# Two reorderings in the recurrence of the odd layer: one on TensorE's queue, one on ScalarE's

## The reference, cut to what matters

```
def _odd_mixer(h_ctx, h_lat, w_in, lower_bounds, layer, out_norm, ctx_out):
    fq, f_fwd, f_bwd, fi, fog = _split(h @ w_in, ODD_SIZES)
    q = _heads(jax.nn.silu(fq), HGRN_HEADS)
    ...
    for d, f in enumerate((f_fwd, f_bwd)):
        log_f = jnp.logaddexp(jnp.log(lb[d]), jnp.log1p(-lb[d]) + jax.nn.log_sigmoid(...f...))
        k = -jnp.expm1(log_f)
        dirs.append(_directional_scan(q, k, i, log_f, n_ctx, reverse=(d == 1)))
    o_lat = _gated_readout(dirs[0][1] + dirs[1][1], og[:, :, n_ctx:], out_norm)
```

## Time and profile before

| | |
|---|---|
| median of three runs | 3188.07 us |
| the profiled execution | 3188.07 us |
| its span, first to last instruction | 3186.1 us |
| TensorE busy | 3034.2 us, 95% of the span |
| VectorE busy | 731.6 us, 23% |
| ScalarE busy | 414.7 us, 13% |
| GpSimd busy | 245.7 us, 8% |
| granted TensorE clock, mean | 0.978 of 2.4 GHz |

### The profile page before, as it was taken

The page is one execution under the profiler, slowest core; times in us unless marked ns, Lnnn a source line. Parts: engine busy times, 40 slices in busy tenths (PEclk is TensorE's granted clock), DMA queues, the critical chain, the costliest instruction groups (busy, mean ns, idle before and its releaser), DMA issues.

```text
span 3186.1 us, 41136 instructions
## 1 busy us (share of the span) xinstructions
PE 3034.2 (95%) x17920; PEld 1710.6 (54%) x17920; DVE 731.6 (23%) x1717; ACT 414.7 (13%) x1014; POOL 245.7 (8%) x322
## 2 busy tenths in 40 slices
PE   6988889999989999899988999989999999999998
PEld 2455644444448888577656777454444444444434
DVE  1037822000035666400032000243000000000002
ACT  1015220000022222200031000131000000000001
POOL 1022300000011122100000000000000000000030
PEclk9999989999999999999999999999999999999999
DMA  8670012122122222243343333326999999999993
GB/s 348 256 279 24 1 66 80 40 99 79 40 62 67 53 63 65 85 168 115 143 172 119 139 139 154 115 85 255 365 399 378 385 400 380 381 403 381 381 404 134
DMA packets 211812, 613.32 MB, mean 192 GB/s; under 512 B 6252, under 2 KB 53580, under 8 KB 205104
## 3 DMA queue, kind: packets, MB, share of 16 engines
q1 hardware_dynamic: 204912, 592.20, 49.0%
q0 software_dynamic: 6256, 17.87, 1.7%
q10 hardware_dynamic: 464, 0.60, 0.1%
HBM read 603.43 MB, written 7.21 MB: 192 GB/s over the span
## 4 chain that ended last, share of the span: by engine, by line
PE 91%; DVE 4%; DMA 2%; issue 1%; ACT 1%; POOLq 0%; POOL 0%; ACTq 0%; DVEq 0%
PE ps_ffn_gate L618 10%; PE ps_ffn_up L618 10%; PE ps_ffn_down L654 10%; PE ps_odd L1921 7%; PE ps_moe_down L3097 6%; PE ps_moe_up L3047 6%; PE ps_moe_gate L3047 6%; PE ps_lin L1408 4%; PE ps_moe_down L3104 3%; PE ps_project L536 3%; PE ps_moe_gate L3052 3%; PE ps_moe_up L3052 3%; PE ps_lin L300 3%; PE ps_odd L1944 2%; PE ps_mod L1331 1%
## 5 line engine op out<-in xcount | busy, mean ns | idle before, releaser
L618 PE MATMUL ps_ffn_gate<-hT,ring_buf 128*128 128x256 f32 (+1 forms) x1152 | 342.4, 451 | 4.3 <-issue 2.3
L618 PE MATMUL ps_ffn_up<-hT,ring_buf 128*128 128x256 f32 (+1 forms) x1152 | 336.7, 445 | 1.3
L654 PE MATMUL ps_ffn_down<-ring_buf,ffn_hiddenT 128*128 128x512 f32 x752 | 326.0, 594 | 3.0 <-issue 3.0
L618 PEld LDWEIGHTS ps_ffn_gate<-hT,ring_buf 128*128 128x128 f32 x1152 | 221.9, 194 | 119.3 <-issue 98.0
L618 PEld LDWEIGHTS ps_ffn_up<-hT,ring_buf 128*128 128x128 f32 x1152 | 218.1, 190 | 110.0 <-issue 89.9
L654 PEld LDWEIGHTS ps_ffn_down<-ring_buf,ffn_hiddenT 128*128 128x128 f32 x752 | 141.9, 190 | 181.8 <-issue 181.8
L1921 PE MATMUL ps_odd<-ring_buf,hT 128*128 128x256 f32 (+2 forms) x1024 | 234.9, 385 | 1.6 <-ACT hg_og_tanh L2054 1.4
L703 DVE TENSOR_TENSOR ffn_hiddenT<-ffn_silu_buf,ps_ffn_up 128x256 f32<-128x256 f32 (+1 forms) x72 | 36.2, 502 | 726.1 <-PE ps_ffn_up L618 726.1
L1921 PEld LDWEIGHTS ps_odd<-ring_buf,hT 128*128 128x128 f32 x1024 | 174.0, 193 | 47.3 <-ACT hg_og_tanh L2054 3.3
L3268 DVE TENSOR_TENSOR moe_hidden_buf<-moe_silu_buf,ps_moe_up 128x768 f32<-128x768 f32 (+1 forms) x32 | 27.3, 854 | 680.8 <-PE ps_moe_up L3052 680.8
L675 ACT ACTIVATE ffn_silu_buf<-ps_ffn_gate 128x256 f32<-128x256 f32 (+1 forms) x72 | 32.3, 449 | 841.8 <-PE ps_ffn_gate L618 841.7
(11 more groups left out here) (556 smaller groups left out, 3376.9 us busy)
## 6 DMA issues: line engine op xcount, KB each, us to landing
ring_buf<-in_w_exp_down_dram SPq DMA_DIRECT2D x17, 4096.0 KB, 18.2
ring_buf<-in_w_exp_up_dram SPq DMA_DIRECT2D x16, 4096.0 KB, 18.5
ring_buf<-in_w_exp_gate_dram SPq DMA_DIRECT2D x15, 4096.0 KB, 19.8
mod_pieces<-in_mod_w_dram SPq DMA_DIRECT2D x40, 1024.0 KB, 6.6
moe_third<-in_w_exp_gate_dram SPq DMA_DIRECT2D x9, 4096.0 KB, 19.7
moe_third<-in_w_exp_up_dram SPq DMA_DIRECT2D x8, 4096.0 KB, 19.2
moe_third<-in_w_exp_down_dram SPq DMA_DIRECT2D x7, 4096.0 KB, 18.2
ring_buf<-in_odd_w_in_dram SPq DMA_DIRECT2D x40, 512.0 KB, 5.3
```

The source lines that it names most:

```text
L618: mm = nc.tensor.matmul(ps[:, 0:wide], view[:, k, i * P:(i + 1) * P], hT[:, k, first_col:first_col + wide], start=k == 0, stop=k == KD - 1)
L654: mm = nc.tensor.matmul(ps_y[i % 2][:, h, :], hidT[:, b, i * P:(i + 1) * P], view[:, b, h * 512:(h + 1) * 512], start=first, stop=end)
```

## The change

There are two edits, both of order alone. On TensorE the projection step `f` 2 of the next head moves behind `scores(u + 1)`; this happens in heads 0 to 6. On ScalarE `logarithms` moves ahead of the takes of `kT` and `fT`; this happens for all 8 heads. No instruction is added or removed on any engine, and the lists of VectorE and GpSimd stay as they are.

```
                     ahead(("f", 1))
                     scores(u)
+                    scores(u + 1)
                     ahead(("f", 2))
-                    scores(u + 1)
                     output(u)
...
                 for kind, t in [("lb", 0)] + PROJECTED:
                     take(0, kind, t)
-                for kind, t in TURNED[:2]:
-                    take(0, kind, t)
                 logarithms(0)
-                for kind, t in TURNED[2:]:
+                for kind, t in TURNED:
                     take(0, kind, t)
...
                         for kind, t in PROJECTED[2:]:
                             take(h + 1, kind, t)
-                        for kind, t in TURNED[:2]:
-                            take(h + 1, kind, t)
                         logarithms(h + 1)
-                        for kind, t in TURNED[2:]:
+                        for kind, t in TURNED:
                             take(h + 1, kind, t)
```

## The result

The changed kernel took 3210.22 us, the median of four runs (3208.34 to 3210.55); the kernel before, with one more run than was shown, 3187.93 us (3182.32 to 3188.34). The ratio is 1.0069, with a 95% interval of 1.0057 to 1.0081. The forecast was 3205.2 us, with a range up to 3209.0: slower, as forecast, but by 22.3 us and not 17.1, and outside the range. The profiled execution of the changed kernel took 3207.33 us, with a span of 3205.5; the profiled execution before took 3188.07.

What follows compares the result with a forecast made beforehand. TensorE, on the last-ending chain for 91% of the span, was taken to bound the kernel. Added waits of 8.9 us (ScalarE's edit) and 8.2 us (TensorE's) made 17.1: 3188.07 + 17.1 = 3205.2 us, range 3196.5 to 3209.

Steps and rivals of the forecast that it cites:

- contention term of edit two: VectorE's end keys of direction 1, beside GpSimd's later keys: 0.30 us more a head, with bounds 0 and 0.61.
- edit two: TensorE, scores(u + 1) ahead of f 2: waits for VectorE's queries, costing 1.17 us seven times, 8.2 us.
- GpSimd works on for 0.61 of them, in which VectorE does half as much: At VectorE's two end keys: 0.61 us run beside GpSimd at half pace, adding 0.30 us a head.
- Edit one: ScalarE, logarithm ahead of kT and fT: i 1 waits for kT's copy, 1.11 us in 8 heads, 8.9 us.
- the strict form: VectorE's end keys beside GpSimd: reading the shared port as an exclusive lock gives 0.61 us a head, 2.1 us more in all.
- VectorE standing still: Rival at the end keys: VectorE stops while GpSimd works, 7 x 0.31 us more, 3207.3 us; chance 0.07.
- its sign: For VectorE stopping beside GpSimd: a wait of 1.4 us for VectorE at the scores, L1944.
- The dearer table switch: Rival at ScalarE's table load before the logarithm: 1.28 us paid again in 8 heads, 10.2 more, 3215.4 us; chance 0.05.
- the second sum given with it: At ScalarE's table load: the skill's drain of about 1380 ns on top would make the sum 11.0 us higher, 3216.3.
- The faster case: Rival before qT: 0.29 us idle ends a ScalarE data chain that an earlier logarithm starts sooner; at most 7.2 us; chance 0.05.
- nothing behind the mixer starts by the clock, so the delay is passed on whole: Behind the mixer: next-stage weights are fetched when TensorE frees a buffer, so all 17.1 us reach the total.

Runs made afterwards that it cites:

- the cover alone: Kernel before with output(u + 3) moved behind iqo 3 on TensorE, nothing else: 3182.19 us, ratio 0.9986.

## Why the prediction was wrong, point by point

The direction, the two waits, their places and their counts were right: 8 waits of `i` 1 for the `kT` copy, 7 waits of the scores of u + 1 for the queries, no gain anywhere but the 0.05 us at `output(u + 1)`, clock 1.00 in the mixer. Two things put the number off. Inside the mixer the delay was 18.5 us for 17.1; 3188.07 + 18.5 = 3206.6 would have lain in the range. The other 3.8 us stand outside the mixer, for which the sum had nothing.

- **The contention term of edit two was too small, and its rule was wrong.** I had 0.30 us for VectorE's end keys beside GpSimd and 1.12 for the wait. The step that failed is "GpSimd works on for 0.61 of them, in which VectorE does half as much". The end keys begin 0.56 us before GpSimd ends (1088.68 and 1089.24), so the overlap was right. But VectorE does not run at half pace in it: the first end key waits for the end of the GpSimd instruction and takes 0.70 instead of 0.28, which is 0.42 more, and the second takes 0.28 as always. The context keys were the other 0.1: they start earlier against the GpSimd instruction beside them and take 0.99 for 0.91. Together the queries are 0.53 later, and the wait is 1.35. Edit two costs about 1.40 a head and not 1.17: 9.8 us for 8.2.
- **Edit one** measured 1.06 a head for 1.11, because `kT`'s copy takes 0.58 there and not 0.65, and the rest of its steps were right to 0.05 us. It gives 8.5 for 8.9. Together the two terms make 18.3 of the mixer's 18.5, for 17.1 forecast.
- **The range left out the scatter of the kernel.** I took three runs within 0.5 us, and a profiled execution equal to their median, as the precision of the measurement, and gave the range only the doubts of my sum. Single executions spread by 2.8 us (standard deviation over 18 runs of the kernel before), and a median of four against four can be off by 3 us. With all runs the difference is 20.2 and not 22.3, so somewhat over half of the 3.8 us is that scatter. The 1.7 us left, at an error of 1.4, stay open. In hindsight a range of 3197 to 3213 would have said what was known.

The reading behind the failed step was one of the earlier trace rows. The 0.93 us of two end keys beside GpSimd is no factor two in each. One by one, in the last head before the change, they are:

```profile
1304.03 0.70 POOL L1847 TENSOR_TENSOR ring_buf<-ring_buf,rec_block_products 128x256 f32<-128x256 f32 x1
1304.16 0.72 DVE L2194 TENSOR_TENSOR rec_k_end<-hg_k_buf,rec_rest_decay 128x128 f32<-128x128 f32 x1
1304.80 0.28 DVE L2194 TENSOR_TENSOR rec_k_end<-hg_k_buf,rec_rest_decay 128x128 f32<-128x128 f32 x1
```

The first ends 0.15 us behind the GpSimd instruction, and the second is not slowed. With that, the prediction's own times give 1084.46 + 0.14 - 1083.85 = 0.75 for the first end key, 0.47 more than 0.28 and not 0.30. The sentence that the trace does not agree with the strict form was wrong too. What the Trainium skill (SBUF — State Buffer, SBUF: two separate sides) calls "an exclusive lock, not a bandwidth split" agrees with these rows, and with the GpSimd instruction that took 1.24 us behind VectorE's context keys.

Of the rivals, VectorE standing still (3207.3) was the nearest in number, and its mechanism was the right one for the length of a GpSimd instruction; its sign, a wait of 1.4 us, was met by 1.35. It was priced a little too high, since it took the whole 0.61 for lost. The dearer table switch is refuted by 1.30 us from load to logarithm in its new place (the second sum given with it should read 3216.2, not 3216.3). The faster case is refuted twice: the logarithm 1 us earlier started nothing earlier, and the 0.29 us before `qT` were a drain. The step "nothing behind the mixer starts by the clock, so the delay is passed on whole" stands within the error: 17.3 us of plain work gave 16.3 (2.6).

## What to carry to other kernels

Before moving a step ahead on the engine that bounds, read off when its inputs are ready: here the queries were ready 0.77 us after the new place and 2.7 us before the old one, and the moved step had been the cover. When an off-path engine starts later, ask what it then runs beside: GpSimd's keys ended 1.9 us later and cost VectorE's critical stretch 0.5 us; 2.3 us later, they cost 1.1. Before taking a pace from a row that merges several instructions, ask for them one by one: the two end keys of 0.93 us were one of 0.72 and one of 0.28. Read the spread of single executions from a dozen runs before setting a range, and read an edit's size from the length of its own stage.

## What was unexpected of the hardware

- VectorE and GpSimd, both in tensor_tensor instructions that read SBUF twice, hold each other up by whole instructions. A 128x256 product of VectorE that begins beside one of GpSimd's key instructions ends 0.27 to 0.29 us behind it (0.72 to 0.95 us instead of 0.41 to 0.45), a 128x128 end key 0.14 to 0.15 behind it (0.70 to 0.72 instead of 0.28). Where VectorE began 0.03 us ahead, it was GpSimd's instruction that took 1.24 us instead of 0.74. GpSimd hardly pays otherwise: its last three keys of direction 1 take 2.23 to 2.31 us in every kernel that makes them.
- A drain of TensorE with a signal shows as 0.26 us of idle time and costs 0.43 in the mixer, where a signal on the next matmul costs nothing that can be seen. With 74 of them gone the kernel is about 14 us faster than with the cover alone.
- Two executions of one program, equal to 0.1 us in a stage with TensorE always busy, differ by 6.6 us in all; 3.8 of them arise in one stretch of many short waits, at a granted clock of 0.91 in the one and 0.99 in the other.
